# Four modulation blocks weighed on GpSimd from two small buffers, and the first layer's order beside it

## The reference, cut to what matters

```
c_act = silu(c)                                   # 1 x 1024
for layer in range(2):
    mod = c_act @ ada_w[layer] + ada_b[layer]     # 1 x 6144: sh1, sc1, g1, sh2, sc2, g2
    h = rms_norm(x, norm_mix_g[layer]) * (1 + sc1) + sh1
    y = mlstm_moba_mixer(h, ...) if layer == 0 else diff_attention_mixer(h, ...)
    x = x + g1 * y
    h = rms_norm(x, norm_ffn_g[layer]) * (1 + sc2) + sh2
    x = x + g2 * peer_ffn(h, ...)
...
# first mixer: z = h @ w_in; mLSTM over 4 heads with a sigmoid output gate,
# and causal attention over 8 heads whose q and k are rms-normed per head; then y @ w_out
```

## Time and profile before

| | |
|---|---|
| median of 3 runs | 2338.02 us (2333.70 to 2341.77) |
| the profiled execution | 2334.95 us, its span 2333.1 us |
| mean granted TensorE clock | 0.851 of full |
| PE / PEld / DVE / ACT / POOL busy | 77% / 36% / 56% / 37% / 28% |
| DMA | 925.71 MB, mean 397 GB/s |
| chain that ended last | DMA 46%, PE 35%, DVE 9%, ACT 5%, issue 3%, POOL 1% |

### The profile page before, as it was taken

The page is one execution under the profiler, slowest core; times in us unless marked ns, Lnnn a source line. Parts: engine busy times, 40 slices in busy tenths (PEclk is TensorE's granted clock), DMA queues, the critical chain, the costliest instruction groups (busy, mean ns, idle before and its releaser), DMA issues.

```text
span 2333.1 us, 30743 instructions
## 1 busy us (share of the span) xinstructions
PE 1789.5 (77%) x11142; PEld 840.8 (36%) x11142; DVE 1297.3 (56%) x3199; ACT 852.9 (37%) x2292; POOL 656.0 (28%) x604
## 2 busy tenths in 40 slices
PE   6999877696786777588778667777779997666666
PEld 3554522161352333154335112333337553222222
DVE  4878887678647766856876867456542321111111
ACT  1224354444445544444744435434333420000000
POOL 1002444434334433433434544333330300000000
PEclk9999986696798888689979766878989999787888
DMA  9988899999999999999999999999997389999998
GB/s 393 372 341 324 321 421 421 420 420 419 399 421 421 420 420 421 419 391 421 420 418 421 421 420 421 421 420 416 414 378 280 138 353 428 428 428 428 429 428 377
DMA packets 110861, 925.71 MB, mean 397 GB/s; under 512 B 12774, under 2 KB 14340, under 8 KB 17732
## 3 DMA queue, kind: packets, MB, share of 16 engines
q0 software_dynamic: 76800, 549.70, 57.3%
q1 hardware_dynamic: 33924, 374.26, 38.9%
HBM read 922.81 MB, written 6.06 MB: 398 GB/s over the span
## 4 chain that ended last, share of the span: by engine, by line
DMA 46%; PE 35%; DVE 9%; ACT 5%; issue 3%; POOL 1%; SPq 0%; DVEq 0%; POOLq 0%
DMA arena<-in_peer_uv_dram,arena 26%; DMA arena<-in_moe_pieces_dram 14%; PE summed L1462 7%; DVE y_g L2947 5%; PE gp L1051 4%; DMA mod<-in_w_parts_dram 3%; PE gp L1538 3%; PE gp L1065 2%; PE gp L1844 2%; PE gp L1056 2%; DMA arena<-in_w_parts_dram 2%; PE gp L1667 1%; PE gp L1434 1%; PE gp L1534 1%; ACT arena L2189 1%
## 5 line engine op out<-in xcount | busy, mean ns | idle before, releaser
L1462 PE MATMUL summed<-arena 64*64 64x512 f32 x4096 | 692.8, 774 | 330.7 <-ACT arena L2189 305.2
L2947 DVE CUSTOM_DVE_ANT_0 y_g<-arena,h 128x1024 f32<-128x1024 f32 x512 | 627.4, 1225 | 404.0 <-DMA arena<-in_peer_uv_dram,arena 339.4
L991 POOL DMA_INDIRECT arena<-in_peer_uv_dram,arena x512 | 592.2, 1157 | 894.8 <-PE summed L1462 813.8
L1462 PEld LDWEIGHTS summed<-arena 64*64 64x64 f32 x4096 | 135.1, 157 | 757.3 <-ACT arena L2189 651.3
L2183 ACT ACTIVATE arena<-arena 128x1 f32<-128x1 f32 x512 | 102.7, 201 | 549.7 <-DVE arena L2947 548.7
L1844 PE MATMUL gp<-arena,mod 128*32 128x512 f32 x1008 | 157.7, 762 | 102.0 <-DMA arena<-in_moe_pieces_dram 102.0
L2189 ACT ACTIVATE arena<-cst,arena 128x128 f32<-128x128 f32 x512 | 205.5, 401 | 16.7
L3329 DVE TENSOR_TENSOR mod<-mod,gp 128x512 f32<-128x512 f32 x8 | 5.5, 688 | 356.5 <-ACT mod L2474 356.5
L2186 ACT ACTIVATE arena<-arena 128x1 f32<-128x1 f32 x512 | 150.8, 295 | 16.6
L1844 PEld LDWEIGHTS gp<-arena,mod 128*32 128x32 f32 x1008 | 31.8, 125 | 221.2 <-DMA arena<-in_moe_pieces_dram 162.1
L2474 ACT ACTIVATE mod<-gp 128x512 f32<-128x512 f32 x8 | 4.8, 597 | 251.7 <-PE gp L1844 251.7
(11 more groups left out here) (485 smaller groups left out, 2272.3 us busy)
## 6 DMA issues: line engine op xcount, KB each, us to landing
arena<-in_moe_pieces_dram SPq DMA_DIRECT2D x93, 2048.0 KB, 25.5
arena<-in_w_slots_dram SPq DMA_DIRECT2D x43, 2048.0 KB, 12.1
arena<-in_w_parts_dram SPq DMA_DIRECT2D x48, 1024.0 KB, 8.9
mod<-in_w_parts_dram SPq DMA_DIRECT2D x27, 1024.0 KB, 9.4
arena<-in_peer_uv_dram,arena POOLq DMA_INDIRECT x512, 15.8
t_rep<-t_rows POOLq DMA_DIRECT2D x1, 3066.0 KB, 13.9
arena<-t_rep POOLq DMA_DIRECT2D x1, 2304.0 KB, 14.4
y_g<-in_moe_pieces_dram SPq DMA_DIRECT2D x1, 2048.0 KB, 20.9
```

The costliest lines, as they stand in the source:

```text
L991: pool.indirect_dma_start(rowbuf[b], None, a["peer_uv"].rearrange("l n d -> (l n) d"), bass.IndirectOffsetOnAxis(ap=idx[:, col(n):col(n) + ...
L1462: mm = pe.matmul(op[o:o + HALF, b, :], diag[i:i + HALF, n % DIAGS, i:i + HALF], rowbuf[n % ROWS][i:i + HALF, D + b * 512:D + (b + 1) * 512 ...
L2947: v.tensor_tensor_reduce(y[:, t, :], rowbuf[n % ROWS][:, 0:D], h[:, t, :], 1.0, 0.0, ALU.mult, ALU.add, dots[:, c:c + 1]).then_inc(udot, 1)
```

## The change

- The four `mix` blocks leave the weight stream and TensorE. Their weights get an array of their own in memory (`w_pool`), and GpSimd loads them itself, in quarters of 512 KB (4 KB a partition), into two buffers in turn (`pool_in`, the place of the used modulation rows 0 and 1). It weighs them as VectorE does with the others, but in two instructions per row group, and waits for its own semaphore after nearly each. It starts when the fourth `in0` block is done, after its table loads and ahead of the gate product. The fourth block's sum uses the first one's place, so it waits for TensorE's sum of that.
- TensorE sums each of the four with one matmul (`sum_pool_block`): one before the mLSTM, two between its steps, one after query 0.
- The last two `vec` sums of the first part move from before the mLSTM into it; VectorE's wait for them moves from the mLSTM's start to its first division.
- The T5 table: its three loads are issued first, its products stand between the parts and sums of the `ada` blocks, VectorE's addition in the input norm. Turning the tokens waits for it.
- The head norms of `moba`: squares and sums run inside the last `in0` block.
- Head norms everywhere: heads take rows in the order 0, 64, 32, 96, and a spread reads only the 64-row half that holds its rows. `block2` keeps four squares instead of two, and its sums come four at a time.
- The first query's scores come before the second of two `vec` sums. SP loads query 0's weights after query 7's, and waits for the four GpSimd blocks first, since one buffer lies there.
- Several semaphores are merged into `gates_f` and `gates_mm`.

```diff
-VECS = 20
-MIX_VECS = (12, 13, 14, 15)
-MIX_ORDER = ((0, 0), (1, 0), (0, 1), (1, 1), (2, 0), (3, 0), (2, 1), (3, 1))
+VECS = 16
+POOL_BLOCKS = (4, 5, 6, 7)
...
-    for i in MIX_VECS:
-        vecs[i] = ("mix", vecs[i][1], [("part", vecs[i][2][0][2]), ("fold", *vecs[i][2][0][1:])])
+            for l in range(2) for n in range(12) if (n not in POOL_BLOCKS if l else n >= 4)]
...
-    vec(6)
+    vec(2)
...
+        pool_in = [mod[:, D * b:D * (b + 1)] for b in range(2)]
+        pool_acc = [y_g2[:, 3 * D:3 * D + CH], y_g2[:, 3 * D + CH:4 * D], zbuf[:, 7168:7680], y_g2[:, 3 * D:3 * D + CH]]
+        pool_term = zbuf[:, 7680:8192]
...
-        order += [(mix_slots[k], j) for k, j in MIX_ORDER]
+        order += [("pool", 0)] + [(n, 0) for n in vec_slots[10:12]] + [("pool", 1), ("pool", 2)]
...
-        order += [("query", 0), (vec_slots[16], 0), (vec_slots[17], 0), ("query", 1), (second_out, 1), ("query", 2), (vec_slots[18], 0)]
-        order += [("query", 3), ("query", 4), (vec_slots[19], 0)]
+        order += [("query", 0), (vec_slots[12], 0), (vec_slots[13], 0), ("pool", 3), ("query", 1), (second_out, 1), ("query", 2), (vec_slots[14], 0)]
+        order += [("query", 3), ("query", 4), (vec_slots[15], 0)]
...
-            sync.wait_ge(h_ready, T)
-            load_query(0)
...
+            sync.wait_ge(pool_weighed, len(POOL_BLOCKS))
+            load_query(0)
+            for n in range(vec_slots[14], phase_slots["in2"][0]):
                 load_weights(n)
...
+            def load_pairs(j, kk):
+                b = kk % 2
+                pool.dma_start(pool_in[b], a["w_pool"][j][:, D * kk:D * (kk + 1)]).then_inc(pool_block_in[b], 16)
+            def weigh_blocks():
+                pool.wait_ge(gemm_done, group_end(phase_slots["in0"][3]))
+                load_pairs(0, 0)
+                load_pairs(0, 1)
+                for j in range(len(POOL_BLOCKS)):
+                    m = 12 + POOL_BLOCKS[j]
+                    acc = pool_acc[j]
+                    if j == 3:
+                        pool.wait_ge(gemm_done, group_of["pool", 0] + 1)
+                    for kk in range(4):
+                        w = pool_in[kk % 2].rearrange("p (k c) -> p k c", k=2)
+                        pool.wait_ge(pool_block_in[kk % 2], 16 * (2 * j + kk // 2 + 1))
+                        for k in range(2):
+                            col = cact[:, 2 * kk + k:2 * kk + k + 1]
+                            if kk + k == 0:
+                                link(pool.tensor_scalar(acc, w[:, 0, :], col, None, ALU.mult))
+                                link(pool.tensor_scalar(pool_term[0:24, :], ada_b[:, :], ident[0:24, m:m + 1], None, ALU.mult))
+                                link(pool.tensor_tensor(acc[0:24, :], acc[0:24, :], pool_term[0:24, :], ALU.add))
+                                continue
+                            link(pool.tensor_scalar(pool_term, w[:, k, :], col, None, ALU.mult))
+                            ins = pool.tensor_tensor(acc, acc, pool_term, ALU.add)
+                            if (kk, k) != (3, 1):
+                                link(ins)
+                        n = 4 * j + kk + 2
+                        if n < 4 * len(POOL_BLOCKS):
+                            load_pairs(n // 4, n % 4)
+                    ins.then_inc(pool_weighed, 1)
...
+            weigh_blocks()
             gate_and_square()
             divide_causal()
...
-                        elif grp[0] == "fold":
-                            _, l, m = grp
-                            r = 32 * (m % 4)
-                            pe.wait_ge(gemm_moved, group_of[n, 0] + 1)
-                            pe.matmul(bank[r:r + 1, :], quarter, mix_part[m % 2], start=True, stop=False)
-                            mm = pe.matmul(bank[r:r + 1, :], ident[0:24, 12 * l + m:12 * l + m + 1], ada_b[:, :], start=False, stop=True)
...
+                rows = slice(64 * (norm_row(i) // 64), 64 * (norm_row(i) // 64) + 64)
                 for half in range(2):
-                    r = 32 * j + 16 * half
-                    mm = pe.matmul(tp[64 * half:64 * (half + 1), i % 2, 0:norm_width(stage_name)], ident[:, r:r + 1].to_broadcast([P, 64]),
-                                   norm_scale(stage_name, b), start=True, stop=True)
+                    r = norm_row(i) + 16 * half
+                    mm = pe.matmul(tp[64 * half:64 * (half + 1), i % 2, 0:norm_width(stage_name)], ident[rows, r:r + 1].to_broadcast([64, 64]),
+                                   norm_scale(stage_name, b)[rows, :], start=True, stop=True)
...
-                steps = [((), ()), ((0, 1), ()), ((2, 3), ()), ((4, 5), ()), ((6, 7), (0, 1)), ((8, 9), (2, 3))]
+                steps = [((), ()), ((), ()), ((0, 1, 2, 3), ()), ((), ()), ((4, 5, 6, 7), (0, 1)), ((), (2, 3))]
...
+            def sum_pool_block(j):
+                g = group_of["pool", j]
+                r = 32 * (POOL_BLOCKS[j] % 4)
+                pe.wait_ge(gemm_moved, g - 1)
+                pe.wait_ge(pool_weighed, j + 1)
+                pe.matmul(gp[r:r + 1, g % 2, :], ones1[:, 0:1], pool_acc[j], start=True, stop=True).then_inc(gemm_done, 1)
...
-                mix(0)
                 scores(0)
                 for hh in range(M_HEADS):
                     if hh + 1 < M_HEADS:
                         scores(hh + 1)
-                        mix(2 * hh + 1)
+                        if hh == 0:
+                            project("vec", slice(10, 12))
+                        else:
+                            sum_pool_block(hh)
...
-            project("ada")
+            for i in range(4):
+                project("ada", slice(i, i + 1), tile=0)
+                if i < DIL_GROUPS:
+                    distance_bias(i)
+                project("ada", slice(i, i + 1), tile=1)
...
-                project("in0", slice(m, m + 1))
+                if m < 6:
+                    project("in0", slice(m, m + 1))
+                else:
+                    for t in range(T):
+                        project("in0", slice(m, m + 1), tile=t)
+                        head_sum("moba", 2 * t)
+                        head_sum("moba", 2 * t + 1)
                 if m == 0:
-                    pe.wait_ge(t5_in, 16 * (NA_HEADS + 3))
-                    for g in range(DIL_GROUPS):
-                        mm = pe.matmul((tp if g < 2 else op)[0:DIL_HPG, g % 2, 0:TW], t5_tab[:, g * DIL_HPG:(g + 1) * DIL_HPG], t5_hot,
-                                       start=True, stop=True)
-                    mm.then_inc(t5_mm, 1)
                     gates()
                 if m == 1:
                     gate_columns()
                 project("vec", slice(*VEC_PARTS[m]))
-            for i in range(len(QK["moba"])):
-                head_sum("moba", i)
-            project("vec", slice(10, 12))
+            sum_pool_block(0)
             mlstm()
             causal_attention()
             pe.wait_ge(o_read, 3)
...
-            project("vec", slice(12, 14))
+            project("vec", slice(12, 13))
             pe.wait_ge(keys_m, 1)
             score_part(0, 0, 0)
+            project("vec", slice(13, 14))
+            sum_pool_block(3)
             first_query(1)
```

More of the change, by code:

```diff
@@ L451, in program @@
         acc_done = sem("acc_done")
+        pool_block_in = [sem(f"pool_block_in{b}") for b in range(2)]
+        pool_weighed = sem("pool_weighed")
         bias_in = sem("bias_in")
@@ L518, in program @@
         for (n, _), g in group_of.items():
-            last_group[n if n == "query" else slots[n][0]] = g + 1
+            last_group[n if n in ("query", "pool") else slots[n][0]] = g + 1
         g_n = len(order)
@@ L2392, in _ @@
             for m in range(7):
-                move("in0", slice(m, m + 1))
+                if m < 6:
+                    move("in0", slice(m, m + 1))
+                else:
+                    move("in0", slice(m, m + 1), tile=0)
+                    head_square("moba", 2)
+                    head_square("moba", 3)
+                    move("in0", slice(m, m + 1), tile=1)
+                    head_root("moba", 0)
                 if m == 0:
@@ L2403, in _ @@
                         silu(c)
-            head_norms("moba")
-            move("vec", slice(10, 12))
+                if m == 5:
+                    head_square("moba", 0)
+                    head_square("moba", 1)
+            move_pool_block(0)
             mlstm()
@@ L2555, in input_norm @@
                             ins.then_inc(h_ready, 1)
+                    if half == 0:
+                        v.wait_ge(t5_in, 48)
+                        v.wait_ge(t5_mm, DIL_GROUPS)
+                        for g in range(DIL_GROUPS):
+                            ins = v.tensor_tensor(t5_mask[:, g * TW:(g + 1) * TW], t5_mask[:, g * TW:(g + 1) * TW],
+                                                  (tp if g < 2 else op)[0:DIL_HPG, g % 2, 0:TW], ALU.add)
+                        link(ins)
+                        v.sem_inc(t5_sum, 1)
             def modrow(i):
```

(7 more changed lines are left out.)

139 lines of the change are left out of this document (67 added, 72 removed).

## The result

The changed kernel takes 2382.85 us (median of 4 runs, 2381.29 to 2384.38) against 2337.48 us (4 runs) before: ratio 1.0199, 95% interval 1.0186 to 1.0211. It is slower by 45 us. The prediction was 2352 with a range up to 2371: the direction held, the forecast shift (+14) was three times too small, and the result lies outside the range. The profiled execution has a span of 2382.5 us against 2333.1, +49.4.

The account below looks back on a forecast made before the run. DMA bytes bound the gathering; before it the first layer's chain, mostly TensorE, counts, where GpSimd would delay the gate product. +19.0 - 0.75 - 4.4 = +13.9 us on 2338.0 gives 2352, range 2328 to 2371.

Parts of the forecast that it names:

- G: Start of the output gate product on GpSimd in the first layer, forecast at 208; later work shifts with it, +19.0 us.
- the own work of GpSimd: GpSimd's instructions and load issues for weighing a mix block: 18.2 us a block, 4.55 per load, with tensor_scalar at 0.80.
- a GpSimd tensor_scalar far from 0.8: Sign named beforehand that would show the forecast wrong: GpSimd's one-input product not taking about the assumed 0.80 us.
- the supply: GpSimd's 512 KB loads beside SP's stream: 7.5 us each until about 172, fourth block weighed at 208.
- Natural gate product: Gate product start in the first layer if nothing else held it, from the TensorE and head norm edits: 166.5 us.
- The port: Rival: VectorE's and GpSimd's weighing hinder each other in the first layer; total +20, 2358 us; chance 0.07.
- The last part: Last projection: head norm sums four at a time and spreads in four tiles save 4.4 us, bounds 0 and -6.
- score product: Towards the gathers: the first score product ahead of the second vector sum comes 0.75 us earlier.
- Starved throughout: Rival: SP's stream stays ahead all the way, gate product at 218 to 232, total 2362 to 2376 us; chance 0.13.
- Keeps up: Rival: loads come at GpSimd's own pace, gate product at 186 or 176, total 2330 to 2320 us; chance 0.17.
- evens out: Rival: gate product falls between 189 and 199, total -5 to +5, 2333 to 2343 us; chance 0.13.
- 6.3 us of head norms: First layer: TensorE's hole while ScalarE squares and roots, claimed to go with squares run beside the last block's matmuls.

Follow-up runs that it names:

- the run with all three repairs: Changed kernel with GpSimd's blocks started early, products as tensor_tensor with the column broadcast, and the fourth block behind the divisions: 2376.71 us, ratio 1.0169.
- the first experiment: Changed kernel with GpSimd's 36 tensor_scalar products written as tensor_tensor with the column broadcast: 2374.1 us, ratio 1.0159.

## Why the prediction was wrong

*What held.* That the gate product decides, and how: "the shift of all that follows is G - 189.0". With G = 238.28 this gives 49.3, and the first gather moved by 49.2, the span by 49.4. The direction, the bottleneck engine, and the place in the queue were right.

*The step that failed* is the own work of GpSimd: "I bound it by half of that, 0.52, and by the whole, 1.04, and take 0.80", with 18.2 us a block. From the first data at 110.79 to the last addition's end at 238.20 GpSimd needs 127.4 us. By its lines these are: products 47.7 + 6.4 + 5.2 + 1.6 = 60.9 (foretold 28.8), additions 28.8 + 8.8 + 4.1 + 1.3 = 43.0 (foretold 33.2), issues of loads with their pauses 11.6 (8.8), gaps between linked instructions 4.9 (2.0), and waits for data 7.0. Without the last that is 120.4 us, 30.1 a block, where 72.8 stood. Two thirds of the error are the products: 1.57 us in a quiet stretch and not 0.80. The additions take 1.26 and not 1.04, the figure of a multiplication of two tensors in the earlier trace rows. The bounds were wrong as such: an operation with one tensor input was bounded from above by one with two. Nothing in the trace excluded that it costs more, and the range had no room for it. The prediction named the sign itself, "a GpSimd tensor_scalar far from 0.8".

By it GpSimd's work sets the end, not the supply. I had put the supply's 208 in its place: at 4.55 us of own work for a load the supply is the slower one, at 7.5 it isn't. The run with loads alone (93.6 us from the first issue to the gate, foretold 101.8) confirms the supply's size, the one with arithmetic alone (117.5 of 133.7 us) and the one with the cheaper product (-11.4) confirm which is the larger. The load times foretold (7 to 12 us up to 172) came as well, with a median of 9.7 between 106 and 182.

*Natural gate product.* "166.5" is measured as 177.6. A slip accounts for 0.9: three of the new sums stand ahead of the gate, 2.6 us by the prediction's own 0.86 each, and the sum has 1.7. (Another slip, in the supply: 63 us from 106.2 end at 169, not at "about 172".) This stayed hidden beneath GpSimd's wait, but it would have misled in every version that tried to repair the change: the mLSTM stage is held by loads and VectorE within a few us of where TensorE was.

*The port.* I gave it 0.07 as a rival; it is a part of the truth, and the sum had it at nothing. VectorE's weighing instructions between 80 and 172 us, before and after (63 each, mean ns of one 752 and 981):

```profile
L2730 DVE SCALAR_TENSOR_TENSOR h<-arena,cst,h 128x512 f32<-128x512 f32 x63 | 47.4, 752 | 2.2
```

```profile
L2794 DVE SCALAR_TENSOR_TENSOR h<-arena,cst,h 128x512 f32<-128x512 f32 x63 | 61.8, 981 | 2.2
```

A row of seven takes up to 8.2 us where it took 5.48 (the rival had 14 for a whole weighing instead of 6.9), the last one ends at 170.2 instead of 158.98, and the last input block waited 5.65 us for its load. With GpSimd's loads but not its arithmetic the mean is 773, so the arithmetic is the cause; beside the products in two-tensor form it is 1197. In the changed kernel all that lies in the shadow of GpSimd's 238, but what GpSimd itself loses doesn't: at 1.565 and 1.26 its 36 products and 32 additions would take 56.3 and 40.3, so 7.3 us of the 103.9 are VectorE's doing (products up to 2.12, additions up to 1.51).

The rule of the Trainium skill that the prediction weighed (SBUF — State Buffer, Who interferes with whom: a VectorE instruction with two SBUF inputs contends with a GpSimd one that reads SBUF) agrees with this in kind: both sides lose, 752 to 981 ns and 1.57 to 2.12 us. The other rule weighed there (the Trainium skill's GPSIMD Engine Reference, section 4.1, Engine selection: one-input operations at about line rate) does not fit this case: by it the prediction estimated 0.43 us, the rows show 1.57, and the two-input form takes 1.04.

*The last part.* Foretold -4.4. The spreads and sums do take half (the earlier trace rows have 0.56 for four and 1.01 for eight; after, eight sums take 0.57 and eight spreads 0.59), but from GpSimd's load ahead of that stage (1733.71 before, 1784.53 after) to the end of the span only 1.4 us came. The chain now goes through VectorE's mask (L2673), which waits 4.9 us for its 16 bias loads; that this is what took the rest wasn't tested:

```profile
1796.21 40.23 DMA mod<-na_rep
```

Of the difference between the foretold shift (13.9) and the measured one (49.4), 33.9 of 35.5 us are: gate product 238.3 for 208 (30.3), score product (0.65 less gain), last part (3.0 less gain); the other 1.6 was lost among the gathers (from the first of them to that load 1485.43 us for 1483.81).

*Rivals.* Starved throughout had nearly the right total (2362 to 2376), by the wrong mechanism: that would have been luck. Keeps up and evens out are excluded.

## What to carry to other kernels

Before moving arithmetic to GpSimd, time one instruction of exactly that form, or bound it from above by far more than the nearest other form; four blocks of 17 such instructions made 120 us of what TensorE did in 15. Look at its neighbour as well: the form that was cheaper on GpSimd made VectorE slower, and in the run with all three repairs TensorE waited for VectorE, not for GpSimd. Count the engine's queue to its end: whatever stands behind the moved work, small loads too, and whatever memory its buffers borrow, waits for it, and moving the work back past one of them only uncovers the next. A hole that opens elsewhere (here 6.3 us of head norms) is worth what the next wait in that stage leaves of it, a quarter at most in this case.

## What the runs showed of the hardware that was not expected

- On GpSimd a product of 128x512 f32 with a column of scalars takes 1.57 us as tensor_scalar and 1.04 us as tensor_tensor with the column broadcast; an addition of two such tensors takes 1.26. With 24 rows instead of 128 the times are the same (1.55 and 1.25).
- Beside VectorE's scalar_tensor_tensor in the changed kernel and in the first experiment these become up to 2.12, 1.46 and 1.61, and VectorE's own 0.75 becomes 0.98 in the mean, and 1.20 beside the two-tensor form. With GpSimd only loading it stays at 0.77.
- TensorE's granted clock was 0.97 from 170 to 238 us before (2.4 GHz nearly throughout) and 0.59 after (mostly 1.2 GHz), where TensorE was busy 35% of the time (23.8 of 68 us). In these windows (us, PE, PEld, DVE, ACT, POOL busy, clock, DMA share, GB/s) the first two rows are the changed kernel's, the last the kernel before's:

```profile
112.00:170.00 58.00, 48.81 (x167) 29.07 (x165) 53.24 (x51) 11.18 (x18) 50.86 (x36) 0.94 0.93 376
170.00:238.00 68.00, 23.78 (x98) 14.34 (x98) 18.98 (x52) 13.72 (x25) 59.74 (x47) 0.59 0.41 151
170.00:238.00 68.00, 62.80 (x305) 31.63 (x304) 54.29 (x132) 29.38 (x75) 14.45 (x22) 0.97 0.83 333
```

- The clock fell ahead of the long wait for the third block, not by it: after waits of 0.68 and 2.18 us the six matmuls at 173.53 took 1.65 us instead of 0.94, and a sum pair took 1.86 at 180.50, 1.87 after the 22.73 us of waiting, and 1.02 at full clock. Some 3 us after that wait the work ran at full clock again (0.94 at 215.29). So even short waits in a row can be followed by matmuls that take nearly twice as long.

```profile
173.53 1.65 PE L1436 MATMUL summed<-arena 128*128 128x128 f32 x6 [2.18 <-DVE arena L2860]
180.50 1.86 PE L1379 MATMUL gp<-y_g,ones 128*1 128x512 f32 x2 [1.53 <-POOL y_g L951]
215.29 0.94 PE L1436 MATMUL summed<-arena 128*128 128x128 f32 x6
```

- The same clock makes the start uncertain. The first 16 matmuls take 3.4 to 3.6 us in every profiled execution (1.2 GHz), and the clock rises after the first slot, within the second or within the third: the same 16 take 1.92 at 2.4 GHz. The input projection begins at 41.7 to 50.8 us, nearly all of it for that reason, since the kernels differ little up to there. This is as large as most effects of single edits here, so single profiles are better compared from a common point, and edits by medians.
